# The output gate's projection between TensorE's products of the recurrence, half an item per block of tokens

## The chip, the cores and the metric

One core of a Trainium2 chip runs the kernel. The core has five engines that run side by side: TensorE (PE, matrix products; PEld is its loading of weights), VectorE (DVE), ScalarE (ACT), GpSimd (POOL) and SyncE (SP, which here issues transfers). They meet only at semaphores. The metric is the device time of one execution in microseconds (us), lower is better, as the median of several executions.

## The reference

One layer of a decoder trunk on 1024 tokens of width 1024, in float32. What matters here is its first half:

```python
xn = rmsnorm(h)
proj = xn @ w_in        # [conv value | conv gate | hgrn q | forget | input | output gate g]
# HGRN2, 4 heads of 128, in chunks of 64 tokens:
f = lb + (1 - lb) * sigmoid(z);  log_f = log(f);  k = (1 - lb) * sigmoid(-z);  q = silu(q_in)
# per chunk: inter + intra products with exp(cumsum(log_f)), state carried to the next chunk
o = rmsnorm_per_head(o) * norm_g
o = o * silu(g)         # the output gate
h = h + concat(y_conv, o) @ w_out
```

The second half (product-key retrieval over 16384 experts) and the final norm are not touched.

## The kernel before

The program is a row of stages, each a block with one instruction stream for each engine; a stage starts when all engines have ended the one before. The stages are: input norm (0 to about 59 us), the projections with the convolution (`mixer`, first block, about 59 to 293 us), the recurrence (`mixer`, second block, 294 to 450 us), the norms and the gate (`mixer`, third block, 450 to about 507 us), the output projection, the queries, the selection with the first expert layer, and the combination (to 3223 us).

**Projections.** Activations stand as two float16 parts `xh` and `xl` in `region_x`, weights as `wh` and `wl`. One item is 128 columns of the weights; one half item is that item on 512 tokens: 8 slices of the contraction with three products each (L398 to L400), 24 in all, into one PSUM bank. Items come in turns of two (ring slots s = 0, 1). SP loads an item (L80), ACT makes the high part and scales the rest (L85, L86), POOL subtracts to make the low part (L91). The order of the turns is: conv gate, conv value, forget, (input projection), q, and last the output gate, `G = (8, 10)`, whose results ACT takes through Silu into `gte` (L474, L475). While PE does this, DVE does the depthwise convolution (L553 to L565) and then four scans (L572) of the log decays.

**Recurrence.** It runs over 8 blocks of 128 tokens. In each block: DVE makes the exponents of 6 levels and of `k_end` (L622, L625); ACT takes Exp of them (L690, L691, L693); POOL multiplies the key half (L723) and DVE the query half (L636, L638); PE makes a product per level and head (L746) and one of the diagonal (L749), into PSUM banks `SCORE = (0, 1, 6, 7)` in turn; DVE copies each level under its mask into `att` (L648, seven copies). PE transposes `k_end` (L755), ACT copies it (L702), PE makes the state updates of both chunks (L762), the product with `att` (L768), and the product with the old state for chunk 0 and chunk 1 (L774). Between those two DVE makes the new state (L660), for which the second waits. ACT copies the block's output to `y` (L682). DVE makes the exponents of block n+1 before the states of block n, so DVE's order in a block is: q products, copies, exponents of the next block, states. Its buffers (levels, states and so on) are carved out of `region_x` (L578), over the activations `xh` and `xl`. After the last block POOL scales `gte` by the norm's gain (L731).

**Norms and gate.** PE takes group means (L819) and then sums of squares (L824); ACT squares (L858) and converts the output weights (L840, L841); then come root, reciprocal, spreading (L833), and DVE multiplies by `gte` (L892).

Of the kernel before, what the change touches and what calls it, by code (L numbers as in the profile page):

```python
# [6 lines left out]
P = 128  # L7
# [314 lines left out]
def mixer(nc, ctx, sb, sems, psum, region_x, y, region_k, region_w, ident, group_mean, stat, const_b, const_m,  # L322
# [16 lines left out]
    tmp = [lbs[:, (2 + i) * CG:(3 + i) * CG] for i in range(6)]  # L339

# [14 lines left out]
    BEFORE_V, TURNS, V_ITEMS = A[1], G[1], KC // 2  # L355
# [7 lines left out]
    with nc.Block() as blk:  # L363
        @blk.sync
        def _(sp):
            def load(turn, s):
                ring.load(sp, s, w_stream[ds(turn * 2 + s, 1), :, :])

            sp.dma_start(cm[:, :], const_m).then_inc(masks_in, 16)
            with sp.Fori(1, BEFORE_V) as turn:  # L370
                for s in range(2):

                    sp.wait_ge(w_lo, BASE + item(turn, s, True) - 1)
                    load(turn, s)
# [3 lines left out]
            with sp.Fori(BEFORE_V, TURNS) as turn:  # L378
                for s in range(2):
                    sp.wait_ge(w_lo, BASE + item(turn, s, False) - 1)  # L380
                    load(turn, s)
            sp.wait_ge(masks_in, 16)

        @blk.tensor
        def _(pe):
# [30 lines left out]
            turns(F[1], TURNS, False, V_TURNS)  # L416

        @blk.scalar
        def _(act):
# [54 lines left out]
            slices(G[0], G[0], silu_to(gte), True, False, V_TURNS)  # L474
            slices(G[0] + 1, G[0], silu_to(gte), False, False, V_TURNS)  # L475

        @blk.gpsimd
        def _(pool):
# [25 lines left out]
            with pool.Fori(F[1] + 1, TURNS) as turn:  # L504
                for s in range(2):
                    low(turn, s, False)
# [69 lines left out]
    used = [0]  # L576

    def carve(n):  # L578
        flat = region_x[:, :, :].rearrange("p a n -> p (a n)")
        used[0] += n  # L580
        return flat[:, used[0] - n:used[0]]

    lev = [carve(CG * P).rearrange("p (h t) -> p h t", h=CG) for _ in range(LEVELS)]
    k_end = carve(CG * P).rearrange("p (h t) -> p h t", h=CG)
    q_beg = carve(CG * P).rearrange("p (h t) -> p h t", h=CG)
    k_blk = carve(CG * P).rearrange("p (h t) -> p h t", h=CG)
    v_blk = carve(CG * P).rearrange("p (h t) -> p h t", h=CG)
    att = carve(CG * P).rearrange("p (h t) -> p h t", h=CG)
    k_end_t = carve(CG * P).rearrange("p (h t) -> p h t", h=CG)
    state = [carve(CG * P).rearrange("p (h t) -> p h t", h=CG) for _ in range(2)]  # L590
    decay = carve(3 * CG).rearrange("p (h c) -> p h c", h=CG)

    LV = LEVELS
    SCORE = (0, 1, 6, 7)
# [13 lines left out]
    with nc.Block() as blk:  # L608
        @blk.vector
        def _(dve):  # L610
# [18 lines left out]
            def intra(n):  # L629
# [11 lines left out]
                for l in range(LV + 1):  # L641
                    dve.wait_ge(sc_mm, BASE + n * (LV + 1) + (l + 1))

                    dve.wait_ge(sc_ok, BASE + n * (LV + 1) + l)

                    dve.memset(decay[:, 0:1, 2:3], 0.0)
                    mask = cm[:, l * P:(l + 1) * P].rearrange("p (a t) -> p a t", a=1).to_broadcast([P, CG, P])
                    dve.copy_predicated(att, mask, bank(SCORE[l % 4])).then_inc(sc_ok, 1)  # L648

# [27 lines left out]
        def _(act):  # L677
# [5 lines left out]

            def decays(n, first):
# [9 lines left out]
                if not first:  # L694
                    outputs(n - 1)
# [8 lines left out]
            decays(0, True)  # L704
            with act.Fori(1, TB) as n:
                decays(n, False)
# [3 lines left out]
        def _(pool):  # L710
            begin(pool, [k_mul])
            with pool.Fori(0, TB) as n:
# [15 lines left out]
                pool.tensor_tensor(k_end, k_end, k_blk, ALU.mult).then_inc(k_mul, 1)  # L728

            for c in range(CG):  # L730
                pool.tensor_scalar(gte[:, c, :], gte[:, c, :], param("hgrn_g")[:, c:c + 1], XS, ALU.mult, ALU.mult)  # L731

        @blk.tensor
        def _(pe):
            begin(pe, [sc_mm, kt_mm, u_mm, o_mm])
            pe.wait_ge(init, BASE + 1)
            with pe.Fori(0, TB) as n:
                q_blk = qry[:, :, ds(n * P, P)]
                for l in range(LV + 1):
# [3 lines left out]
                    pe.wait_ge(sc_ok, BASE + n * (LV + 1) + max(l - 3, 0))  # L743
                    for hh in range(CG):
                        if l < LV:
                            last = pe.matmul(bank(SCORE[l % 4])[:, hh, :], lev[l][:, hh, :], lev[l][:, hh, :],  # L746
                                             start=True, stop=True)
                        else:
                            last = pe.matmul(bank(SCORE[l % 4])[:, hh, :], k_blk[:, hh, :], q_blk[:, hh, :],  # L749
                                             start=True, stop=True)  # L750
                    last.then_inc(sc_mm, 1)
                pe.wait_ge(k_mul, BASE + n * (LV + 2) + (LV + 2))
# [18 lines left out]
                for c in range(2):  # L771
                    pe.wait_ge(s_ok, BASE + 2 * n + c)
# [31 lines left out]
    with nc.Block() as blk:  # L804
# [73 lines left out]
        def _(dve):  # L878
# [1017 lines left out]
```

## Time and profile before

| | us |
|---|---|
| median of 3 runs | 3220.35 (3216.92 to 3223.66) |
| the profiled execution | 3224.61 |
| its span | 3222.8 |
| PE busy | 2946.5 (91%) |
| DVE busy | 2117.0 (66%) |
| POOL busy | 1718.9 (53%) |
| ACT busy | 1109.0 (34%) |

The profiled execution is one of its own: 1.8 us of it lie outside the span, and it is 4.3 us above the median of the runs. The shares are averages over stages with different limits, so each stage is to be read by itself. "PEclk" is the clock that TensorE was granted as a share of full speed (2.4 GHz); it takes two levels, 1.00 and 0.50 (1.2 GHz), and a value between them is a mean over a stretch. A float32 product leaves two matmul records, so the four heads of one level are eight records.

### The profile page before, as it was taken

How to read it: one execution, taken by the hardware profiler on the slowest of the kernel's cores; microseconds unless marked ns; L12 is line 12 of the kernel's file. 1: busy time of each engine (PE TensorE's matmuls, PEld its weight loads, DVE VectorE, ACT ScalarE, POOL GpSimd, SP SyncE). 2: the span in 40 equal slices, each digit the busy share in tenths (PEclk: the TensorE clock that was granted, in tenths of full speed). 3: DMA queues.
4: the chain of work that ended last, by engine and by line, in shares of the span. 5: the costliest groups of instructions: out<-in, count | busy, mean ns of one | idle time of the engine just before them, and what ended most of it. 6: DMA issues, size and time to landing. Idle time of an engine off the chain costs nothing. (4 is left out here: it accounts for less than half of the span.)

```text
span 3222.8 us, 47024 instructions
## 1 busy us (share of the span) xinstructions
PE 2946.5 (91%) x15880; PEld 1644.7 (51%) x15880; DVE 2117.0 (66%) x3995; ACT 1109.0 (34%) x1480; POOL 1718.9 (53%) x1490
## 2 busy tenths in 40 slices
PE   6998779899999999899999999599989979999987
PEld 3444754455555555577777766244434424444333
DVE  2598964211777778677777753477777757777767
ACT  4333353222444444355555553221212211121212
POOL 1213442011444443455555557677887876777884
PEclk9999788999999999999999999799999989999999
DMA  3200012111333333377777777899999996999996
GB/s 114 74 26 14 0 53 85 40 39 39 105 109 114 114 114 109 126 278 249 273 249 271 249 276 248 274 321 328 334 337 340 331 327 244 322 319 326 320 323 236
DMA packets 260395, 648.59 MB, mean 201 GB/s; under 512 B 16992, under 2 KB 115552, under 8 KB 257136
## 3 DMA queue, kind: packets, MB, share of 16 engines
q1 hardware_dynamic: 186176, 378.33, 33.4%
q0 software_dynamic: 74160, 269.52, 23.6%
q8 instruction: 32, 0.52, 0.1%
q14 instruction: 27, 0.22, 0.0%
HBM read 542.39 MB, written 105.91 MB: 201 GB/s over the span
## 5 line engine op out<-in xcount | busy, mean ns | idle before, releaser
L91 POOL TENSOR_TENSOR w_low<-w_ring,w_high 128x1024 f16<-128x1024 f32 x164 | 367.4, 2241 | 1040.6 <-ACT w_ring L86 1040.5
L1664 PE MATMUL psum<-vh,wh 128*128 128x512 bf16 x1536 | 598.5, 390 | 142.5 <-POOL wl L1713 108.9
L1245 PE MATMUL psum<-region_y,w_high 128*128 128x384 f16 x2048 | 672.6, 328 | 18.1 <-POOL w_low L91 16.4
L1246 PE MATMUL psum<-region_y,w_high 128*128 128x384 f16 x2048 | 670.3, 327 | 0.0
L1247 PE MATMUL psum<-region_y,w_low 128*128 128x384 f16 x2048 | 670.3, 327 | 0.0
L1665 PE MATMUL psum<-vl,wh 128*128 128x512 bf16 x1536 | 597.3, 389 | 0.0
L1666 PE MATMUL psum<-vh,wl 128*128 128x512 bf16 x1536 | 596.4, 388 | 0.0
L1680 ACT ACTIVATE vh<-w_ring 128x1024 bf16<-128x1024 f32 x128 | 134.9, 1054 | 896.6 <-DMA w_ring<-in_v_t_dram 836.4
L1775 DVE TENSOR_TENSOR region_x<-region_x,psum 128x1024 f32<-128x1024 f32 x192 | 234.0, 1219 | 153.7 <-PE psum L1666 122.1
L1664 PEld LDWEIGHTS psum<-vh,wh 128*128 128x128 bf16 x1536 | 153.3, 100 | 344.4 <-issue 147.3
L1709 POOL TENSOR_TENSOR vl<-w_ring,vh 128x1024 bf16<-128x1024 f32 x128 | 272.8, 2132 | 40.9 <-ACT vh L1680 40.4
L1297 ACT ACTIVATE ge<-psum 128x384 f32<-128x384 f32 x256 | 125.8, 491 | 476.9 <-PE psum L1247 472.0
L1522 DVE SCALAR_TENSOR_TENSOR tk_work<-tk_work,tk_sc 128x1024 f32<-128x1024 f32 x128 | 207.4, 1623 | 118.3 <-DMA tk_work<-in_u_rows_dram,u_step_rows 117.4
L1245 PEld LDWEIGHTS psum<-region_y,w_high 128*128 128x128 f16 x2048 | 202.8, 99 | 147.9 <-issue 23.3
L1247 PEld LDWEIGHTS psum<-region_y,w_low 128*128 128x128 f16 x2048 | 201.0, 98 | 134.5 <-issue 2.9
L1246 PEld LDWEIGHTS psum<-region_y,w_high 128*128 128x128 f16 x2048 | 202.8, 99 | 126.9 <-issue 2.4
L1666 PEld LDWEIGHTS psum<-vh,wl 128*128 128x128 bf16 x1536 | 153.6, 100 | 191.6 <-issue 18.4
L1665 PEld LDWEIGHTS psum<-vl,wh 128*128 128x128 bf16 x1536 | 153.4, 100 | 186.4 <-issue 16.0
L1338 ACT ACTIVATE scores<-psum 128x512 f32<-128x512 f32 x192 | 189.8, 1095 | 138.3 <-PE psum L1277 138.3
L1713 POOL TENSOR_TENSOR wl<-at,wh 128x768 bf16<-128x768 f32 x128 | 212.3, 1659 | 1.8 <-ACT wh L1683 1.8
L1277 PE MATMUL psum<-scores 128*128 128x128 bf16 x1536 | 196.7, 296 | 4.6 <-DVE scores L1487 4.6
L1753 DVE SCALAR_TENSOR_TENSOR psum<-region_y,weight,psum 128x1024 f32<-128x1024 f32 x128 | 164.6, 1286 | 40.8 <-DMA region_y<-in_v_t_dram,step_rows 31.6
(235 smaller groups left out, 4960.3 us busy)
## 6 DMA issues: line engine op xcount, KB each, us to landing
w_ring<-in_u_t_dram SPq DMA_DIRECT2D x128, 512.0 KB
w_ring<-in_v_t_dram SPq DMA_DIRECT2D x128, 512.0 KB
acts_dram<-ge SPq DMA_DIRECT2D x128, 384.0 KB
gates_dram<-scores SPq DMA_DIRECT2D x24, 2048.0 KB
gt<-gates_dram SPq DMA_DIRECT2D x32, 1536.0 KB, 9.5
at<-acts_dram SPq DMA_DIRECT2D x32, 1536.0 KB, 13.5
w_ring<-in_w_stream_dram SPq DMA_DIRECT2D x20, 512.0 KB, 3.2
w_ring<-in_w_q_dram SPq DMA_DIRECT2D x16, 512.0 KB, 3.3
```

Source lines behind the costliest of these rows:

```text
L91: pool.tensor_tensor(self.wl[:, s, :], self.wf[:, s, :], self.wh[:, s, :], ALU.subtract).then_inc(self.w_lo, 1)
L1245: pe.matmul(a, uh[:, par, row], xh[:, n, cols], start=(n == 0), stop=False)
L1246: pe.matmul(a, uh[:, par, row], xl[:, n, cols], start=False, stop=False)
L1247: last = pe.matmul(a, ul[:, par, row], xh[:, n, cols], start=False, stop=(n == KC - 1))
L1277: last = pe.matmul(psum[:, 4 + 2 * r + b, t * P:(t + 1) * P], hot[:, r, 0, b, :, t], hot[:, r, part, b, :, t], start=(part == 2), stop=(pa ...
L1522: dve.scalar_tensor_tensor(out=row[:, r, :], in0=row[:, r, :], scalar=1.0, in1=xtok[:, :], op0=ALU.mult, op1=ALU.mult, accum_out=dots[:, j ...
L1664: pe.matmul(a, wh[:, par, c, rows], vh[:, par, c, cols], start=(c == 0), stop=False)
L1665: pe.matmul(a, wh[:, par, c, rows], vl[:, par, c, cols], start=False, stop=False)
L1666: last = pe.matmul(a, wl[:, par, c, rows], vh[:, par, c, cols], start=False, stop=(c == CPG - 1))
L1709: pool.tensor_tensor(vl[:, par, c, :], vf[:, c % 2, :], vh[:, par, c, :], ALU.subtract).then_inc(v_lo, 1)
L1713: pool.tensor_tensor(wl[:, par, c, :], at[:, par, c, :], wh[:, par, c, :], ALU.subtract).then_inc(w_lo, 1)
L1775: dve.tensor_tensor(a, a, banks, ALU.add).then_inc(y_ok, 1)
```

## The change

The output gate's two turns leave the projections. In the recurrence, PE does half an item (24 products) per block of tokens, 8 half items in 8 blocks: three products behind each of the first four levels, and twelve between the state products of chunk 0 and chunk 1. They go to PSUM bank 7, which the scores give up (`SCORE = (0, 1, 6)`). ACT copies the bank into `gte` without Silu (`gates`), one block later, before that block's output; Silu over all of `gte` comes after the last block, before the last output's copy. The items of turn 9 are loaded by SP at the start of the recurrence and converted by ACT and POOL behind blocks 2 and 4. POOL no longer scales `gte`; it scales the four columns of the gain, and DVE applies them with the gate in one instruction. Since `xh` and `xl` have to live on, the recurrence's buffers move to `glu` and to new ones. ACT's, POOL's and PE's loops over blocks are written out.

```diff
-    BEFORE_V, TURNS, V_ITEMS = A[1], G[1], KC // 2
+    BEFORE_V, V_ITEMS = A[1], KC // 2
...
-            turns(F[1], TURNS, False, V_TURNS)
+            turns(F[1], G[0], False, V_TURNS)
...
-            slices(G[0], G[0], silu_to(gte), True, False, V_TURNS)
-            slices(G[0] + 1, G[0], silu_to(gte), False, False, V_TURNS)
...
-    SCORE = (0, 1, 6, 7)
+    SCORE = (0, 1, 6)
+    NS = len(SCORE)
+    G_BANK = 7
...
+        @blk.sync
+        def _(sp):
+            for s in range(2):
+                ring.load(sp, s, w_stream[2 * (G[0] + 1) + s:2 * (G[0] + 1) + s + 1, :, :])
...
+            def gates(n):
+                _, _, c, cols = gate_half(n)
+                act.wait_ge(g_mm, n + 1)
+                act.activation(gte[:, c, cols], psum[:, G_BANK, :], ACT.Copy, scale=BACK).then_inc(g_out, 1)
...
                 if not first:
+                    gates(n - 1)
                     outputs(n - 1)
...
-            decays(0, True)
-            with act.Fori(1, TB) as n:
-                decays(n, False)
+            for n in range(TB):
+                decays(n, n == 0)
+                if n in (NH, 2 * NH):
+                    ring.high(act, n // NH - 1, G[0] + 1 + V_ITEMS // 2)
+            gates(TB - 1)
+            act.wait_ge(g_out, TB)
+            for c in range(CG):
+                act.activation(gte[:, c, :], gte[:, c, :], ACT.Silu)
             outputs(TB - 1)
...
-            for c in range(CG):
-                pool.tensor_scalar(gte[:, c, :], gte[:, c, :], param("hgrn_g")[:, c:c + 1], XS, ALU.mult, ALU.mult)
+                if n in (NH, 2 * NH):
+                    s = n // NH - 1
+                    ring.low(pool, s, item(G[0] + 1, s, False))
+            pool.tensor_scalar(hgrn_gain, param("hgrn_g"), XS, None, ALU.mult)
...
+            def gate_part(n, first, end):
+                turn, s, _, cols = gate_half(n)
+                if first == 0:
+                    pe.wait_ge(w_lo, BASE + item(turn, s, False) + 1)
+                    if n:
+                        pe.wait_ge(g_out, n)
+                for k in range(first, end):
+                    row = slice(k * P, (k + 1) * P)
+                    pe.matmul(psum[:, G_BANK, :], wh[:, s, row], xh[:, k, cols], start=(k == 0), stop=False)
+                    pe.matmul(psum[:, G_BANK, :], wh[:, s, row], xl[:, k, cols], start=False, stop=False)
+                    last = pe.matmul(psum[:, G_BANK, :], wl[:, s, row], xh[:, k, cols], start=False,
+                                     stop=(k == KC - 1))
+                if end == KC:
+                    last.then_inc(g_mm, 1)
...
-                    pe.wait_ge(sc_ok, BASE + n * (LV + 1) + max(l - 3, 0))
+                    pe.wait_ge(sc_ok, BASE + n * (LV + 1) + max(l + 1 - NS, 0))
...
                     last.then_inc(sc_mm, 1)
+                    if l < KC // 2:
+                        gate_part(n, l, l + 1)
...
                 for c in range(2):
+                    if c == 1:
+                        gate_part(n, KC // 2, KC)
                     pe.wait_ge(s_ok, BASE + 2 * n + c)
...
-                    dve.tensor_tensor(at(y, (c, h)), at(y, (c, h)), at(gte, (c - CG, h)),
-                                      ALU.mult).then_inc(gated_ok, 1)
+                    dve.scalar_tensor_tensor(out=at(y, (c, h)), in0=at(y, (c, h)),
+                                             scalar=hgrn_gain[:, c - CG:c - CG + 1], in1=at(gte, (c - CG, h)),
+                                             op0=ALU.mult, op1=ALU.mult).then_inc(gated_ok, 1)
```

How the change orders the work on PE. First the levels of a block in the kernel before (L746 is a level's four heads, L749 the diagonal, L755 the transposes; `REGISTER_ALU` and `ISA` compute the loop's addresses):

```order
508 L746 MATMUL psum<-region_x 128x128 x4
509 L741 REGISTER_ALU
510 L742 REGISTER_ALU
511 L746 MATMUL psum<-region_x 128x128 x4
512 L741 REGISTER_ALU
513 L742 REGISTER_ALU
514 L746 MATMUL psum<-region_x 128x128 x4
```

Then the same place in the changed kernel (its L781 is the level, L765 to L767 the gate's products):

```order
504 L781 MATMUL psum<-glu 128x128 x4
505 L765 MATMUL psum<-region_x,w_high 128x512
506 L766 MATMUL psum<-region_x,w_high 128x512
507 L767 MATMUL psum<-region_x,w_low 128x512
508 L781 MATMUL psum<-glu 128x128 x4
509 L765 MATMUL psum<-region_x,w_high 128x512
```

Three products of 512 columns now stand between a level and the next, four times in a block. Second, ACT behind the last block, in the kernel before (L702 is the copy of the transposed `k_end`, L682 the output's copy, L858 the first squares of the next stage):

```order
171 L702 ACTIVATE region_x<-psum 128x512
172 L705 REGISTER_ALU
173 L705 COMPARE_AND_BRANCH
174 L682 ACTIVATE region_y<-psum 128x4x128
175 L608 UNCONDITIONAL_BRANCH
176 L836 UNCONDITIONAL_BRANCH
177 L858 ACTIVATE region_x<-region_y 128x1024 x4
```

and in the changed kernel (L712, L686 and L897 are those three; L691 is `gates`, L722 the Silu):

```order
263 L712 ACTIVATE hg_rest<-psum 128x512
264 L691 ACTIVATE gte<-psum 128x512
265 L722 ACT_TABLE_LOAD
266 L722 ACTIVATE gte<-gte 128x1024 x4
267 L686 ACTIVATE region_y<-psum 128x4x128
268 L607 UNCONDITIONAL_BRANCH
269 L875 UNCONDITIONAL_BRANCH
270 L897 ACTIVATE region_x<-region_y 128x1024 x4
```

Six instructions come to stand ahead of the last output's copy. Third, POOL behind block 2, in the changed kernel (L744 ends block 2's work, L91 is the ring's low part, L733 starts block 3):

```order
64 L744 TENSOR_TENSOR glu<-glu,hg_rest 128x512
65 L91 TENSOR_TENSOR w_low<-w_ring,w_high 128x1024
66 L733 COPY hg_rest<-region_k 128x512
67 L739 TENSOR_TENSOR glu<-glu,hg_rest 128x8x32
68 L739 TENSOR_TENSOR glu<-glu,hg_rest 128x16x16
```

In the kernel before, nothing stands between the first and the third of these; L91 of the output gate's items ran in the projections.

## Rows read from the trace of the kernel before

**Rows 1.** Windows: stretch, length, busy of PE, PEld, DVE, ACT, POOL; PEclk, DMA, GB/s

```profile
251.40:292.30 40.90, 40.88 (x190) 18.34 (x188) 33.50 (x24) 10.02 (x14) 8.49 (x3) 1.00 0.04 13
312.30:424.80 112.50, 86.13 (x600) 82.70 (x600) 101.73 (x218) 39.39 (x102) 57.94 (x54) 0.82 0.00 0
450.10:471.10 21.00, 20.94 (x48) 5.95 (x48) 5.49 (x8) 17.21 (x18) 8.52 (x4) 1.00 0.42 145
476.60:504.50 27.90, 27.64 (x32) 10.46 (x32) 22.61 (x30) 17.81 (x26) 15.93 (x11) 0.50 0.06 19
```

**Rows 2.** Timeline, DVE and ACT: start, us, instruction, count [idle before <-releaser]

```profile
274.19 10.71 DVE L572 TENSOR_TENSOR_SCAN region_k<-restart,region_k 128x1024 f32<-128x1024 bf16 x4
293.82 0.48 DVE L665 MEMSET region_x<- 128x512 f32 x1 [8.92 <-PEq L363]
292.32 0.60 ACT L445 ACTIVATE gte<-psum 128x512 f32<-128x512 f32 x1 [4.58 <-PE psum L400]
```

**Rows 3.** Timeline of DVE over two blocks, and the stage's last two copies

```profile
377.59 2.10 DVE L636 TENSOR_TENSOR region_x<-region_x,region_w 128x256 f32<-128x256 f32 x6
387.24 5.28 DVE L622 TENSOR_TENSOR region_x<-region_k 128x512 f32 x6
393.59 2.32 DVE L660 SCALAR_TENSOR_TENSOR region_x<-region_x,psum 128x128 f32<-128x128 f32 x8
395.83 3.59 DVE L636 TENSOR_TENSOR region_x<-region_x,region_w 128x256 f32<-128x256 f32 x6
399.94 0.72 DVE L648 COPY_PREDICATED region_x<-cm,psum 128x512 f32<-128x512 int32 x1
406.55 4.15 DVE L622 TENSOR_TENSOR region_x<-region_k 128x512 f32 x5
443.51 0.73 DVE L648 COPY_PREDICATED region_x<-cm,psum 128x512 f32<-128x512 int32 x1
444.37 0.72 DVE L648 COPY_PREDICATED region_x<-cm,psum 128x512 f32<-128x512 int32 x1
```

**Rows 4.** Timeline of PE: state updates, last product with the state, levels

```profile
387.78 1.71 PE L762 MATMUL psum<-region_x 64*128 64x128 f32 x16 [0.77 <-ACT region_x L702]
394.75 1.10 PE L774 MATMUL psum<-region_x 128*128 128x64 f32 x8 [3.34 <-DVE region_x L660]
396.48 8.51 PE L746 MATMUL psum<-region_x 128*128 128x128 f32 x48 [0.62 <-DVE region_x L636]
```

**Rows 5.** Windows of granted clock: levels at half and at full, and two gaps

```profile
396.50:402.20 5.70, 5.70 (x27) 5.70 (x28) 5.08 (x12) 0.72 (x3) 1.62 (x2) 0.50 0.00 0
402.60:406.30 3.70, 3.70 (x34) 3.48 (x32) 2.70 (x9) 0.00 (x0) 0.24 (x1) 1.00 0.00 0
1070.40:1078.00 7.60, 5.28 (x33) 3.22 (x34) 7.11 (x17) 4.64 (x5) 4.17 (x2) 1.00 0.34 121
1266.00:1272.80 6.80, 4.46 (x18) 2.22 (x18) 6.17 (x12) 4.18 (x4) 4.33 (x3) 0.76 0.39 135
```

**Rows 6.** Timeline of POOL and DVE in the first block

```profile
296.23 6.57 POOL L723 TENSOR_TENSOR region_x<-region_x 128x256 f32<-128x256 f32 x6 [1.99 <-ACT region_x L691]
301.05 4.86 DVE L636 TENSOR_TENSOR region_x<-region_x,region_w 128x256 f32<-128x256 f32 x6
```

**Rows 7.** Timeline of ACT and POOL: the ring's conversions and a table load

```profile
273.04 1.05 ACT L86 ACTIVATE w_ring<-w_ring 128x1024 f32<-128x1024 f32 x1
274.16 4.23 POOL L91 TENSOR_TENSOR w_low<-w_ring,w_high 128x1024 f16<-128x1024 f32 x1 [8.23 <-ACT w_ring L86]
210.05 1.28 ACT L470 ACT_TABLE_LOAD   x1
```

**Rows 8.** Timeline of PE and ACT: end of the recurrence, start of the norm stage

```profile
447.26 1.90 PE L774 MATMUL psum<-region_x 128*128 128x64 f32 x16
449.19 0.60 ACT L682 ACTIVATE region_y<-psum 128x512 f32<-128x512 f32 x1 [4.70 <-PE psum L774]
450.08 3.90 ACT L858 ACTIVATE region_x<-region_y 128x1024 f32<-128x1024 f32 x4 [0.29 <-PEq L608]
```

More of the change, by code:

```diff
@@ L339, in mixer @@
     tmp = [lbs[:, (2 + i) * CG:(3 + i) * CG] for i in range(6)]
+    hgrn_gain = tmp[0]
     masks_in = sems("masks_in")
@@ L377, in _ @@
                 sp.dma_start(wf[:, j % 2, :], w_v[j, :, :]).then_inc(w_in[j % 2], 16)
-            with sp.Fori(BEFORE_V, TURNS) as turn:
+            with sp.Fori(BEFORE_V, G[0] + 1) as turn:
                 for s in range(2):
@@ L503, in _ @@
                                    ALU.mult, ALU.mult).then_inc(key_ok, 1)
-            with pool.Fori(F[1] + 1, TURNS) as turn:
+            with pool.Fori(F[1] + 1, G[0] + 1) as turn:
                 for s in range(2):
@@ L572, in _, with gate_half @@
                 dve.tensor_tensor_scan(logf[:, c, :], restart[:, :], logf[:, c, :], 0.0, ALU.mult, ALU.add)
[L576 to L591, printed above, removed]
-    LV = LEVELS
-    SCORE = (0, 1, 6, 7)
+    in_glu = glu[:, :, :].rearrange("p c n -> p (c n)")[:, 0:8 * CG * P].rearrange(
+        "p (i h t) -> p i h t", i=8, h=CG)
+    hg_rest = sb(ctx, "hg_rest", [P, 6, CG, P], F32)
+    lev = [in_glu[:, i] for i in range(LEVELS)]
+    k_end, q_beg = in_glu[:, LEVELS], in_glu[:, LEVELS + 1]
+    k_blk, v_blk, att, k_end_t = (hg_rest[:, i] for i in range(4))
+    state = [hg_rest[:, 4 + i] for i in range(2)]
+    decay = sb(ctx, "hg_decay", [P, CG, 3], F32)
+    LV = LEVELS
+    SCORE = (0, 1, 6)
+    NS = len(SCORE)
+    G_BANK = 7
+    g_mm, g_out = sems("gate_mm"), sems("gate_out")
+    def gate_half(n):
+        c, h = divmod(n, NH)
+        return G[0] + c // 2, c % 2, c, slice(h * HALF, (h + 1) * HALF)
     init = sems("hg_init")
@@ L647, in intra @@
                     mask = cm[:, l * P:(l + 1) * P].rearrange("p (a t) -> p a t", a=1).to_broadcast([P, CG, P])
[L648 removed]
+                    dve.copy_predicated(att, mask, bank(SCORE[l % NS])).then_inc(sc_ok, 1)
             def states(n):
@@ L711, in _ @@
             begin(pool, [k_mul])
-            with pool.Fori(0, TB) as n:
+            for n in range(TB):
                 kb = key[:, :, ds(n * P, P)]
@@ L736, in _ @@
             pe.wait_ge(init, BASE + 1)
-            with pe.Fori(0, TB) as n:
+            def gate_part(n, first, end):
[12 more added lines that the diff above has]
+                    last.then_inc(g_mm, 1)
+            for n in range(TB):
                 q_blk = qry[:, :, ds(n * P, P)]
@@ L742, in _ @@
                         pe.wait_ge(k_mul, BASE + n * (LV + 2) + (l + 2))
-                    pe.wait_ge(sc_ok, BASE + n * (LV + 1) + max(l - 3, 0))
+                    pe.wait_ge(sc_ok, BASE + n * (LV + 1) + max(l + 1 - NS, 0))
                     for hh in range(CG):
                         if l < LV:
-                            last = pe.matmul(bank(SCORE[l % 4])[:, hh, :], lev[l][:, hh, :], lev[l][:, hh, :],
+                            last = pe.matmul(bank(SCORE[l % NS])[:, hh, :], lev[l][:, hh, :], lev[l][:, hh, :],
                                              start=True, stop=True)
                         else:
-                            last = pe.matmul(bank(SCORE[l % 4])[:, hh, :], k_blk[:, hh, :], q_blk[:, hh, :],
+                            last = pe.matmul(bank(SCORE[l % NS])[:, hh, :], k_blk[:, hh, :], q_blk[:, hh, :],
                                              start=True, stop=True)
                     last.then_inc(sc_mm, 1)
+                    if l < KC // 2:
+                        gate_part(n, l, l + 1)
                 pe.wait_ge(k_mul, BASE + n * (LV + 2) + (LV + 2))
```

## The prediction

> **What bounds the kernel now.** I read the time stage by stage, since the change touches the projections, the recurrence and the start of the norm stage. First the windows [rows 1]: in 251.4 to 292.3 us PE does nothing but the output gate's turns, 190 of its 192 products recorded in 40.9 us, 0.215 us each, at clock 1.00. Then the timeline at the hand-over [rows 2]: DVE's scans end at 274.19 + 10.71 = 284.90, ACT's last Silu at 292.32 + 0.60 = 292.92, and the recurrence starts at 293.82. So PE bounds the end of this stage, but DVE (convolution and scans) is only 8.0 us behind it. Of 41 us taken off PE the stage can give back 8.0.
>
> Then the recurrence. The six blocks from 312.3 to 424.8 take 112.5 us, 18.75 each; DVE is busy 101.7 of it, PE 86.1 with 100 records a block, at a mean clock of 0.82 [rows 1]. I call T the moment at which the states of a block are done and its q products start, and E the start of the next block's exponents. On DVE [rows 3], E to T is 387.24 to 395.83 = 8.6 us; T to E is 377.59 to 387.24 = 9.65 us in one block and 395.83 to 406.55 = 10.72 in the next, so periods of 18.2 and 19.3 alternate. In the longer one the q products take 3.59 us against 2.10.
>
> On PE [rows 4], the product with the new state waits 3.34 us for DVE: there the twelve gate products fit. The levels start 0.65 us after T (396.48). Their pace depends on the clock [rows 5]: at 0.50, 27 records in 5.70 us, 0.211 each; at 1.00, 34 in 3.70, 0.109 each. A level is eight records: 1.7 us or 0.9. After the 3.34 us gap the levels ran at half clock for 5.7 us; after the 0.77 us wait for ACT the state updates (L762, 16 records in 1.71, 0.107 each) went on at full [rows 4].
>
> **The change part by part**, as differences to the profiled execution.
>
> *Projections, -8.0.* The gate's turns go; late next is DVE's last scan. With the same 0.9 us from the last instruction to the next stage, the recurrence starts at 285.8 instead of 293.82 [rows 2]. This is nearly certain: -7.5 to -8.5.
>
> *Does the clock hold?* In each block PE gets 12 products x 0.215 = 2.6 us into the 3.34 us gap, and 4 x 3 x 0.215 = 2.6 us among the levels. Its work per block at full clock is 100 x 0.109 + 5.2 = 16.1 of about 19 us, and the waits left are 0.77 (ACT), 0.7 before the state product and 0.62 before the levels [rows 4]. The 0.7: PE ended chunk 0's product at 394.75 - 3.34 = 391.4, E + 4.2; with 2.6 more it is E + 6.8, and the state, which DVE starts at 393.59 [rows 3], is there at 394.75, E + 7.5. Two gaps of about 2 us in another stage bracket this: around 1070.4 to 1078 the mean clock stayed 1.00, in 1266 to 1272.8 it fell to a mean of 0.76 [rows 5]. Mine are shorter than both, so I take the clock as held from block 1 on.
>
> *Score phase, blocks 1 to 6: +1.5.* At full clock: first level at T + 0.65; seven products (six levels and diagonal) x 0.9 = 6.3; four gate groups x 0.65 = 2.6; so PE ends at T + 9.55, the last copy (0.72, [rows 3]) starts about 0.15 later, and E = T + 10.4. DVE by itself would take, with the slower q products, 395.83 to 399.94 = 4.1 and seven copies at the pitch of 444.37 - 443.51 = 0.86: 10.1. PE is late by a little. The period is 8.6 + 10.4 = 19.0 against 18.75: +0.25 x 6 = +1.5. What full clock gives is spent on the gate groups. With three score banks instead of four, level 3 waits for copy 0, done at T + 4.1 + 0.7 = 4.8; PE reaches level 3 at T + 0.65 + 2.7 + 1.95 = 5.3, so this costs nothing; if PE were 0.5 us quicker it would bind. Bounds: -0.75 per block (all like the 9.65 block, [rows 3]), that is -6 over eight blocks, and for the other end rival B.
>
> *Block 0: +2.4.* PE has stood idle since the projections, so it starts at half clock, as before (0.50 over levels, [rows 5]). A stretch of 5.7 us at half costs half of it, 2.85; with 0.4 for the first q product beside POOL [rows 6], T to E is 10.4 + 2.85 + 0.4 = 13.65; before it was 301.05 [rows 6] to 312.3, 11.25. Bounds 0 and +3.5.
>
> *ACT and POOL at blocks 2 and 4: +2.0.* The ring's two ACT passes are 1.05 each, and POOL's subtraction 4.23 / 2 = 2.1 [rows 7]. POOL waits for ACT's, and block n+1's key products (6.57 us, [rows 6]) queue behind POOL's: they start some 4 us later and run on past T. PE doesn't wait for them, since level l needs only product l. But DVE's q products then run beside them: 4.86 us as in block 0 [rows 6] instead of 3.59, +1.27, of which the 0.3 that DVE is ahead of PE absorbs some: +1.0, twice. Bounds 0 (hidden) and +2 x 2.1 (POOL's whole subtraction shows). ACT's 2.1 us lie in its waiting (ACT is busy 39 of 112.5 us, [rows 1]); `gates`, 0.6 a block, runs while ACT waits for the output (4.70 us idle behind block 7, [rows 8]). The two loads fall where DMA moves nothing [rows 1]: nothing.
>
> *Behind block 7: +7.2.* Nothing hides anything here. Before: PE's two state products back to back from 447.26, 1.90 for both; ACT's copy 449.19 + 0.60 = 449.79 ends the stage [rows 8]. After: first product to 448.2; twelve gate products, +2.6 = 450.8; `gates` 0.6 = 451.5 with a tenth for the semaphore; table load 1.28 [rows 7] = 452.8; four Silu of 128x1024, as the four squares 3.90 [rows 8] = 456.7; the output's copy 0.6 = 457.3. That is +7.5, less 0.3 because PE's last levels end earlier at full clock. Bounds +6 and +8.5.
>
> What the Trainium skill says of the table load speaks for more: its page "ScalarE: Activation LUTs", section "What ACT_TABLE_LOAD costs", puts a drain beside the load, about 2.7 us for a switch. The row shows 1.28 for the load alone, and by the page this term would be +8.6 instead of +7.2.
>
> *Norm stage: +2.4.* PE does 48 records in 21.0 us without a pause and the root waits for the last [rows 1]; at the start, before, the clock was full. Now PE idles from its last product (about 451.7 on the old scale) to 457.6, more than any gap above that held, so it starts at half: half of 5.7 us = 2.85, less about 0.4 in which ACT was the later one. Bounds +1.3 and +3.4. The gating on DVE takes one more scalar per instruction, cost nothing: PE is busy 27.6 of 27.9 us there at clock 0.50, DVE 22.6 [rows 1]; without that cover 8 x 0.1 us. POOL's L731 goes from a stretch where PE, at half clock, was the later one: nothing.
>
> Sum: -8.0 + 1.5 + 2.4 + 2.0 + 7.2 + 2.4 = **+7.5**. Against the profiled 3224.6 us that is 3232.1; that execution is 4.3 above the median of 3220.35, so the median forecast is 3227.9. A difference under 0.2% (6.4 us) can't be told from none.
>
> **Rivals.**
>
> *B, the clock still falls in the recurrence.* Place: PE between chunk 0's state product and the next levels. If the waits left add up so that the clock drops as before, the levels and the gate groups run at half for 5.7 us of each such block, +2.85: in every second block +10, in all seven +20, so 3238 to 3248. For it: the 1266 window, where a gap of about 2 us was enough [rows 5]. Against it: my gaps are about 0.7 each. The Trainium skill ("TensorE: Matmul & The Clock Gate", section "A second HAM failure mode: psum-queue depth-cycling") tells of a kernel whose frequent short PE pauses made the clock swing, without one long one; the held 1070 window speaks against it here. Chance 0.17.
>
> *C, not slower: DVE carries the score phase.* Place: L746 to the last copy. In the full-clock levels PEld is busy 3.48 of 3.70 us [rows 5], so a gate product's 0.215 us may cover the next float32 weight load and a group cost 0.4 instead of 0.65. It decides once the last level ends before T + 9.2; then E is DVE's 10.1 (-0.3 x 8 = -2.4), and if the q products also take the short form, 9.65: -0.75 x 8 = -6.0, and the ring's 2.0 gone. 3220 to 3225.5, at best 3219.9. Against it: full clock lets POOL start its copies right at T, as in the longer blocks. Chance 0.23.
>
> *A, the sum above,* 0.60; its own range is 3222 to 3234 by its terms, 0.38 of it beyond +6.4 and 0.22 within.
>
> **Numbers.** Slower: 0.38 + 0.17 = 0.55. Same: 0.22 + 0.15 of C = 0.37. Faster: 0.08, the low end of C with a cheaper tail. The range 3217 to 3240 holds A, nearly all of C and the near half of B.
>
> **What would show it.** Right: the recurrence begins at about 286; block periods near 19.0 without alternation; mean clock near 1.00 over blocks 1 to 6; blocks 3 and 5 about 1 us longer; PE's wait before the state product about 0.7; table load and four Silus, some 7 us, between PE's last product and the next stage; PE at 0.50 as that starts. Wrong: a clock of 0.8 or less in the blocks and periods over 21 (B); periods of 18.5 or less with no copy waiting for PE (C); the term for the tail under 5, or a first norm stretch at clock 1.00.

## The result, and the profile after

| kernel | median (us) | runs | profiled execution | its span |
|---|---|---|---|---|
| before | 3221.0 | 8 (3216.9 to 3223.7) | 3224.61 | 3222.8 |
| after | 3229.2 | 8 (3226.4 to 3234.4) | 3234.42 | 3232.6 |

The ratio is 1.0027, with a 95% interval of 1.0016 to 1.0038: 8.2 us slower, where 7.5 was forecast. The profiled executions' spans differ by 9.8 us, and that is the sum taken apart here; the profiled one of after is the slowest of its eight, 5.2 us above their median. Medians were taken on four occasions, and the kernel before measured 3221.0, 3222.9, 3227.7 and 3223.8 us on them. So runs of different occasions are compared by their ratios to it, and not by their medians.

The windows of the changed kernel (columns as in [rows 1]) show one block with a fall of the clock (block 1), one without (block 6), six blocks together, the tail, and the norm stage's start; the last two are the stretch at half clock in block 1, and the levels behind it:

```profile
305.20:325.70 20.50, 18.53 (x124) 14.66 (x124) 17.62 (x38) 7.17 (x19) 9.16 (x10) 0.92 0.00 1
408.60:427.40 18.80, 16.87 (x124) 13.60 (x124) 17.60 (x37) 7.13 (x19) 9.13 (x10) 1.00 0.00 1
305.20:427.40 122.20, 109.41 (x744) 87.35 (x744) 109.35 (x217) 45.97 (x113) 58.45 (x57) 0.93 0.00 1
427.40:459.30 31.90, 23.93 (x176) 19.09 (x176) 19.99 (x45) 13.82 (x26) 8.93 (x10) 0.99 0.00 1
459.50:482.00 22.50, 22.44 (x46) 6.93 (x47) 5.50 (x8) 18.39 (x19) 9.38 (x5) 0.87 0.41 143
...
315.40:318.70 3.30, 3.30 (x14) 2.33 (x13) 3.22 (x7) 0.00 (x0) 0.67 (x1) 0.51 0.00 0
319.00:323.90 4.90, 4.90 (x40) 4.33 (x39) 2.57 (x7) 0.00 (x0) 0.00 (x0) 1.00 0.01 3
```

The six blocks took 122.2 us where they took 112.5 [rows 1], and DVE's busy time grew with them (101.7 to 109.4). Nearly all of that is in the q products: 17.1 us in the six blocks before, where three blocks had the short ones of 2.10, and 24.8 us now, where none has. The mean clock rose from 0.82 to 0.93, but not to the 1.00 on which the forecast counted: it fell once in each of blocks 1 to 5, to 0.51 (the 1.2 GHz level) for about 3.3 us, and the period (from the start of a block's exponents to the next block's) was 20.5 us, with the ring's work 21.0; block 6, without a fall, took 18.8.

On DVE, the scans, the recurrence's first instruction, the q products of three blocks, and the starts of blocks 2 and 7:

```profile
274.86 8.83 DVE L571 TENSOR_TENSOR_SCAN region_k<-restart,region_k 128x1024 f32<-128x1024 bf16 x4
284.60 0.48 DVE L669 MEMSET hg_rest<- 128x512 f32 x1 [0.91 <-PEq L364]
...
313.78 3.58 DVE L640 TENSOR_TENSOR glu<-glu,region_w 128x256 f32<-128x256 f32 x6
321.73 0.73 DVE L652 COPY_PREDICATED hg_rest<-cm,psum 128x512 f32<-128x512 int32 x1 [0.81 <-DVE hg_rest L652]
325.69 5.28 DVE L626 TENSOR_TENSOR glu<-region_k 128x512 f32 x6
...
354.96 5.21 DVE L640 TENSOR_TENSOR glu<-glu,region_w 128x256 f32<-128x256 f32 x6
...
427.43 5.28 DVE L626 TENSOR_TENSOR glu<-region_k 128x512 f32 x6
```

The recurrence begins at 284.60 instead of 293.82 [rows 2]: 9.2 us earlier. The 0.81 us idle before the copy at 321.73, though put down to DVE's own buffer, is time in which no levels were there to copy: PE was at half clock until 318.7, and a level with its gate group takes it 1.54 us even after that (the copies at 320.19, 321.73 and 323.27 are that far apart). The q products of block 3 take 5.21 us.

PE around the gap of block 2, whose clock fell at 335.75:

```profile
333.19 1.10 PE L813 MATMUL psum<-glu,hg_rest 128*128 128x64 f32 x8 [0.83 <-DVE hg_rest L664]
334.74 1.23 PE L781 MATMUL psum<-glu 128*128 128x128 f32 x8 [0.45 <-DVE glu L640]
```

Of the 3.34 us before the product with the state [rows 4], 0.83 is left (0.7 was forecast); 0.45 before the levels. Blocks 1, 4, 6 and 7 have the same two waits within 0.01 us, and in blocks 6 and 7 the clock held; blocks 3 and 5, with the ring's work, have 1.04 and 0.78.

The tail and the start of the norm stage, on ACT:

```profile
452.97 0.60 ACT L691 ACTIVATE gte<-psum 128x512 f32<-128x512 f32 x1 [6.32 <-PE psum L767]
453.58 1.28 ACT L722 ACT_TABLE_LOAD   x1
454.88 3.89 ACT L722 ACTIVATE gte<-gte 128x1024 f32<-128x1024 f32 x4
458.68 0.57 ACT L686 ACTIVATE region_y<-psum 128x512 f32<-128x512 f32 x1
459.53 3.89 ACT L897 ACTIVATE region_x<-region_y 128x1024 f32<-128x1024 f32 x4 [0.28 <-PEq L607]
...
479.07 1.06 ACT L879 ACTIVATE region_w<-w_ring 128x1024 f16<-128x1024 f32 x1 [1.90 <-DMA w_ring<-in_w_out_dram]
482.58 0.59 ACT L902 ACTIVATE glu<-psum 16x512 f32<-16x512 f32 x1 [0.21 <-PE psum L863]
```

Block 7 starts at 427.43 and the norm stage 32.1 us later; before it was 424.78 and 25.3. Nothing covers the load, the four Silu and the copy. The root comes 23.05 us into the stage, before 22.6.

### The profile page after: what moved, and what is told of

Read it like the earlier page. It is cut to its first block and busy times, and to the rows that moved or that the text cites. A ratio compares the mean times of both kernels' runs of the same rounds, so it can differ in the third digit from the quotient of the medians.

```text
span 3232.6 us, 46622 instructions
## 1 busy us (share of the span) xinstructions
PE 2941.5 (91%) x15880; PEld 1633.5 (51%) x15880; DVE 2123.6 (66%) x3995; ACT 1112.7 (34%) x1485; POOL 1712.0 (53%) x1487
## 5 line engine op out<-in xcount | busy, mean ns | idle before, releaser
L91 POOL TENSOR_TENSOR w_low<-w_ring,w_high 128x1024 f16<-128x1024 f32 x164 | 364.0, 2220 | 1049.0 <-ACT w_ring L86 1049.0
```

Of the source, the lines that this page charges most:

```text
L91: pool.tensor_tensor(self.wl[:, s, :], self.wf[:, s, :], self.wh[:, s, :], ALU.subtract).then_inc(self.w_lo, 1)
```

## The experiments

The diffs are shortened to the lines that matter. The main theory, H: PE's clock falls at the waits that are left and costs 1.65 us a time; with the waits filled it holds. Its rival: the new order itself makes the blocks 20.5 us long. "Behind E7" is the time from block 7's start to the norm stage, E and T are the prediction's.

**e1: three more products in each gap.** They are repeats and compute nothing that is used.

```diff
  gate_part(n, KC // 2, KC)
+ for _ in range(3):
+     pe.matmul(psum[:, 2, :], wh[:, gate_half(n)[1], 0:P],
+               xh[:, 0, 0:HALF], start=True, stop=True)
```

> The changed kernel with three more products of 512 columns (0.65 us) that nobody uses, into PSUM bank 2, in PE's wait before the state product of chunk 1 (0.82 us in the profile). Theory H: in blocks 1 to 5 the clock fell for 3.3 us of each block because of the waits left around the state product (0.82 and 0.44 us), and each fall costs half of 3.3 us. Then with the wait filled the clock stays at 1.00 in all blocks, the periods of 20.5 become 18.8 as in block 6, and the time falls by 5 x 1.65 = 8 us (about 3221). Rival P: the 20.5 is the order of PE's work (levels queue behind gate products) and the clock a by-product; then periods stay 20.5 and the time the same within 2 us.

Measured: 3226.1 us, ratio 1.0014 (1.0005 to 1.0023), with more work on PE than in after. Its six blocks, and PE in blocks 2 and 3:

```profile
303.38:419.69 116.31, 105.58 (x762) 83.25 (x762) 109.32 (x217) 46.00 (x113) 58.47 (x57) 1.00 0.00 1
```

```profile
329.70 1.11 PE L815 MATMUL psum<-glu,hg_rest 128*128 128x64 f32 x8 [0.17 <-DVE hg_rest L664]
331.25 0.94 PE L781 MATMUL psum<-glu 128*128 128x128 f32 x6 [0.44 <-DVE glu L640]
...
356.42 1.13 PE L781 MATMUL psum<-glu 128*128 128x128 f32 x8 [0.91 <-DVE hg_rest L652]
```

With 0.17 us left of the wait (0.39 in the ring's blocks) the clock is 1.00 in all six blocks, and four of the six periods are 18.8. H stands, and the order of work alone (P) is out. The other two, with the ring's work, are 20.5: there PE waits 0.91 us for DVE to copy a score bank. So the ring costs 1.7 us a time where the clock is held; in after it showed as 0.5, beside a fall. That is why the six blocks are only 5.9 us shorter than in after's profile (116.31 for 122.2) and not 8. In the median, expected about 3221, it is less still: from a ratio of 1.0027 to 1.0014, about 4 us, and the two intervals overlap.

**e2: seven eighths of the Silu before the end**, in ACT's wait of block 7.

```diff
+ if last:        # behind block 7's decay
+     act.wait_ge(g_out, TB - 1)
+     # Silu of gte[:, 0:CG-1, :] and gte[:, CG-1, 0:HALF]
...
- # gates(TB - 1), four Silu of 128x1024
+ act.activation(gte[:, CG - 1, HALF:T], psum[:, G_BANK, :], ACT.Silu, scale=BACK)
```

> The changed kernel with seven of the eight halves of Silu (and the table load) taken while ACT waits for the transposes in the last block (8.8 us idle), and the last half directly from PSUM. Theory T: behind the last block nothing hides ACT, so table load 1.28 and Silu 3.9 are paid in full: the stage end comes 5.2 us earlier, time -5.2; PE's pause before the norm stage shrinks from 6 to about 1.5 us, so that stage may start at full clock and give back up to 1.7 more. Rival: what comes earlier is lost in the norm stage's waits for the output weights, time the same within 2 us.

Measured: 3227.8 us, ratio 1.0020 (1.0011 to 1.0029). ACT in the tail:

```profile
436.73 1.28 ACT L713 ACT_TABLE_LOAD   x1
438.02 2.95 ACT L713 ACTIVATE gte<-gte 128x1024 f32<-128x1024 f32 x3
440.88 0.61 ACT L714 ACTIVATE gte<-gte 128x512 f32<-128x512 f32 x1
...
452.38 0.60 ACT L725 ACTIVATE gte<-psum 128x512 f32<-128x512 f32 x1 [6.32 <-PE psum L770]
453.22 0.60 ACT L686 ACTIVATE region_y<-psum 128x512 f32<-128x512 f32 x1 [0.24 <-PE psum L816]
```

Behind E7 it is 27.25 us instead of 32.1: 4.85 saved (5.2 expected). The ratio is 0.0007 below after's, some 2 us, and the intervals overlap. The tail's size is shown, its whole worth in the total is not.

The second half of the expectation can be read too. Here PE's pause was short and the norm stage ran at full clock from its start to its root:

```profile
454.10:476.97 22.87, 20.94 (x48) 5.99 (x48) 5.51 (x8) 18.76 (x19) 9.76 (x5) 1.00 0.43 141
```

It took 22.87 us, where after's took 23.05 with its first 6 us at half clock. So the fall at this place cost next to nothing, and not the 1.7 that were expected back.

**e3: a smaller share among the levels**, three slices instead of four; five in the gap.

```diff
- if l < KC // 2:      gate_part(n, l, l + 1)
+ if l < IN_LEVELS:    gate_part(n, l, l + 1)      # IN_LEVELS = 3
- gate_part(n, KC // 2, KC)
+ gate_part(n, IN_LEVELS, KC)
```

> The changed kernel with five slices of the gate (15 products, 3.2 us) between the two state products and three among the levels, instead of four and four. Theory H: the wait before the state product shrinks from 0.82 to 0.17 us, the clock holds, and the level phase is 0.65 us shorter, so that DVE bounds it (10.1 us from states to exponents): periods of 18.6, time -8 to -10. Rival P (the order of work alone): -0.65 x 7 = -4.5, periods 19.8, clock still falling.

Measured: 3226.6 us, ratio 1.0007 (0.9998 to 1.0016), not told from before; against after it is some 6 us (the two intervals only touch), where 8 to 10 were expected. The clock is 0.99 over six blocks: it fell once, in block 3, where the ring's work had lengthened the two waits to 1.29 and 0.89 us (block 5 has the same waits, and no fall). Four periods are 18.5, and the two with the ring 21.0 (block 3) and 20.4. T to E is 9.95 us: with one group fewer PE is no longer the late one, and DVE sets the pace (rival C's place).

```profile
304.41:419.96 115.55, 103.12 (x744) 82.25 (x744) 109.48 (x217) 46.83 (x113) 58.61 (x57) 0.99 0.00 1
```

**e4: the kernel before with its gap filled**, by 14 products that compute nothing.

```diff
  for c in range(2):
+     if c == 1:
+         for _ in range(14):
+             pe.matmul(psum[:, 2, :], wh[:, 0, 0:P], wl[:, 0, 0:HALF], start=True, stop=True)
```

> The kernel before with 14 products of 512 columns (3.0 us) that nobody uses, into PSUM bank 2, in PE's 3.34 us wait before the state product; everything else as before. It prices the clock's fall in the kernel before. If levels at half clock hold up DVE's copies there, the periods fall from 18.75 to DVE's own 8.6 + 10.0 = 18.6 or less, clock 1.00: time -1 to -3 us. If the shorter q products of every second block were due to the half clock (POOL starting its copies later), they go as well and the periods become 18.6 all alike. If products in the wait delay the state product, the time rises by 0.3 per block, +2.

Measured: 3224.6 us, ratio 1.0005 (0.9996 to 1.0014).

```profile
312.64:423.75 111.11, 94.13 (x693) 78.47 (x695) 105.71 (x218) 39.92 (x102) 54.64 (x54) 0.97 0.00 0
```

The alternation of 18.2 and 19.3 is gone: every period is 18.5. The clock still fell in blocks 3, 5 and 7, but for 3.4 us instead of 6.8, and these blocks are no longer than the others. How the alternation came about can be read in the trace of the kernel before, at T of block 4 (the state product on PE, and POOL's copy behind it) and of block 5 (POOL's copy):

```profile
376.51 1.97 PE L774 MATMUL psum<-region_x 128*128 128x64 f32 x8 [3.33 <-DVE region_x L660]
```

```profile
378.66 1.49 POOL L726 COPY region_x<-region_w 128x512 f32 x1 [1.74 <-PE psum L774]
396.04 0.67 POOL L726 COPY region_x<-region_w 128x512 f32 x1 [0.88 <-PE psum L774]
```

Where the clock had fallen before the state product, that took 1.97 us instead of 1.10 [rows 4], POOL's copy waited for it and started 1.07 us behind the q products' start (378.66 for 377.59, [rows 3]) instead of 0.21, and the q products, mostly without POOL beside them, took 2.10 us instead of 3.59. Such a block took 18.2 us, less than the 18.5 of e4 without a fall; where the clock fell behind the state product, the levels took 8.5 us [rows 4], and the block 19.3. The clock's fall so helped by holding POOL back, or cost by slowing the levels, depending on where it began. (In e7 the short q products come once more, and that block is not shorter, so this holds for the kernel before only.) The gain of the filled wait over six blocks is only 1.4 us (111.11 for 112.5), and behind E7 the same products show as +2.5 (27.8 for 25.3). Half clock cost the old kernel little, since DVE carried its blocks.

**e6: no ring work in the recurrence.** It leaves out the loads and conversions of turn 9 and uses another turn's weights in its place. One execution only.

```diff
- item(turn, s, False)
+ item(G[0], s, False)     # and ring.high, ring.low, two loads removed
```

> The changed kernel without the loads and conversions of turn 9 in the recurrence; PE uses turn 8's items twice, so half of the gate's values are left out. The two blocks behind the conversions had q products of 5.2 us instead of 3.6 and periods of 21.0 against 20.5 here, and 20.53 against 18.81 where the wait was filled. Theory R: POOL, pushed back by ACT's two passes and its own subtraction, works beside DVE's q products; then all q products are 3.6 and blocks 3 and 5 have the period of their neighbours (20.5 at a falling clock, 18.8 at a held one). Rival: the longer periods come with the position in the clock's rhythm, and stay.

Measured: 3242.5 us, span 3240.7. DVE and POOL in block 3, and the six blocks:

```profile
354.14 3.58 DVE L639 TENSOR_TENSOR glu<-glu,region_w 128x256 f32<-128x256 f32 x6
```

```profile
347.13 6.34 POOL L735 TENSOR_TENSOR glu<-glu,hg_rest 128x256 f32<-128x256 f32 x6 [1.50 <-ACT glu L699]
```

```profile
304.61:427.45 122.84, 111.14 (x744) 88.71 (x744) 105.56 (x217) 42.89 (x109) 54.91 (x55) 0.92 0.00 1
```

Here the clock fell in all seven blocks and every period was 20.5, blocks 3 and 5 too. The q products took 3.58 us instead of 5.21, so it is the ring's work that pushes POOL's key products beside them. Of the 1.6 us that DVE saves, 0.5 shows in the period (20.5 for 21.0), since PE, at half clock, is late anyway, and a sixth fall among the six blocks took more than both gave. The total says nothing about the ring: 2779.5 us of the span lie behind the start of the norm stage, 6.4 more than in after's profile, in code that is the same.

**e5_again: after once more**, no edit.

> The changed kernel itself, once more. In its first profile the clock fell in blocks 1 to 5 and not in 6; in the run with one more subtraction beside the scans, whose blocks have the same code, it held in blocks 1, 2, 3 and 5. If where it falls is chance of the single execution (gaps of 0.82 and 0.44 us lie at the edge), the set of blocks differs here again, with 1.7 us for each: between no fall (a recurrence 8 us shorter than in the first profile) and a fall in all seven. If it is fixed by the code, blocks 1 to 5 fall again.

Measured: 3233.3 us (3225.6 to 3235.0), ratio 1.0031 (1.0021 to 1.0042). Its profile has falls in blocks 1, 2 and 3 only and a span of 3227.4:

```profile
303.96:424.04 120.08, 106.35 (x744) 85.16 (x744) 109.33 (x217) 45.98 (x113) 58.46 (x57) 0.96 0.00 1
```

The same instructions give three falls in one execution and five in another, with the same waits. So the number of falls is a matter of the execution; the waits make a fall possible and do not fix it. The width of its times (8.0 and 9.5 us) can't be put down to the falls: e1, whose profile has none in its blocks, spreads over 12.3 us, and the kernel before over 6.7 to 12 us. (The expectation has the blocks of e8 wrong: there the clock held in blocks 1 to 4.)

**e7: the change by halves.** Turn 9 and half of turn 10's gate work go back to the projections; blocks 0 to 3 alone carry four slices each, in the gap only. No ring work in the recurrence, no tail.

```diff
- gate_part(n, l, l + 1)                 # among the levels
- gate_part(n, KC // 2, KC)              # in the gap
+ if n < 4: gate_part(n, 4 * (n % 2), 4 * (n % 2) + 4)
```

> The changed kernel with six of the eight half items back in the projections (PE is idle there from 252 to 284 us, six halves take 31), through Silu as before, and two left for the recurrence, as 12 products in the wait before the state product of blocks 0 to 3, none among the levels; no conversions in the recurrence; the last item's Silu while ACT waits in block 7. From the terms measured so far: start -8 (scans beside POOL again, 10.7 instead of 8.8, so not -9.2), blocks as in the kernel before or, where the wait is filled, 18.5 instead of 18.75 (-1), no tail, no ring. Time against the kernel before: -9, about 3213. If the gain at the start is given back later, it is 0.

Measured: 3220.7 us (3213.5 to 3221.9), ratio 0.9974 (0.9965 to 0.9984), with 3227.7 for the kernel before on the same occasion. Windows, then ACT at the end:

```profile
304.35:415.74 111.39, 89.74 (x649) 78.82 (x649) 104.67 (x218) 41.29 (x105) 56.09 (x55) 0.92 0.00 1
```

```profile
426.49 1.28 ACT L724 ACT_TABLE_LOAD   x1
427.79 1.06 ACT L724 ACTIVATE gte<-gte 128x1024 f32<-128x1024 f32 x1
...
439.59 0.60 ACT L696 ACTIVATE region_y<-psum 128x512 f32<-128x512 f32 x1 [4.62 <-PE psum L818]
```

Periods are 18.53 to 18.56, once 18.68, though the clock is 0.92 as in e6 (it fell in blocks 1, 4, 5, 6 and 7): with nothing among the levels, a fall costs next to nothing. Behind E7 it is 24.7 us. The start keeps 7.9 of its 9.2 us. This beats both kernels, by 0.26% or about 8 us against before, where 9 were expected.

**e9: e7 with the gaps of all seven blocks filled** by 2 or 14 empty products.

```diff
+ for _ in range(14 if n in (4, 5, 6) else 2 if n < 4 else 0):
+     pe.matmul(psum[:, 2, :], wh[:, 1, 0:P], xh[:, 0, 0:HALF], start=True, stop=True)
```

> The split kernel with products that nobody uses (14 in blocks 4 to 6, two more in blocks 0 to 3) in PE's wait before the state product, so that it is filled in every block but the last. Theory H: clock 1.00 and periods 18.5 in all blocks: 0.25 less in each of three to seven blocks, -1 to -2 against the split kernel, -10 against the kernel before. Rival: no more than the split kernel, since periods with a fallen clock alternate between 18.2 and 19.3 anyway.

Measured: 3217.9 us, ratio 0.9972 (0.9963 to 0.9981).

```profile
304.53:415.78 111.25, 92.67 (x685) 76.37 (x685) 105.86 (x217) 41.32 (x105) 54.99 (x55) 0.98 0.00 1
```

The clock is 0.98 instead of 0.92 (one fall, in block 6), and the six blocks take 111.25 us instead of 111.39: the same. The 1 to 2 us of theory H did not come. The clock mattered only where PE was late.

**e8: a POOL subtraction put back beside the scans** (one execution, on after; its output is not used).

```diff
+ pool.wait_ge(conv, BASE + CG * TAPS)
+ pool.tensor_tensor(gte[:, 0, :], key[:, 0, :], key[:, 1, :], ALU.subtract)
```

> The changed kernel with one more subtraction of 128x1024 on POOL, of values that nobody uses, started when DVE starts its four scans. The scans took 10.71 us before, when POOL made the last low parts beside them (one instruction, 4.23 us instead of 2.1), and 8.83 in the changed kernel, when POOL was idle. Theory S: they slow one another, so the scans take 10 to 11 us here and POOL's subtraction 3 to 4. Rival: the 1.9 us are not POOL's doing (the convolution's end moved, ACT and PE were busy too), and the scans stay at 8.8.

Measured: 3236.8 us, span 3235.0. DVE, then POOL, then a subtraction of the same size 10 us ahead of the scans, in the kernel before:

```profile
274.96 10.93 DVE L573 TENSOR_TENSOR_SCAN region_k<-restart,region_k 128x1024 f32<-128x1024 bf16 x4
```

```profile
275.12 4.26 POOL L507 TENSOR_TENSOR gte<-region_k 128x1024 f32<-128x1024 f32 x1 [17.94 <-DVE region_y L566]
```

```profile
263.80 2.13 POOL L91 TENSOR_TENSOR w_low<-w_ring,w_high 128x1024 f16<-128x1024 f32 x1 [8.14 <-ACT w_ring L86]
```

One POOL instruction makes the scans 2.1 us longer (8.83 to 10.93), as much as such a subtraction takes away from them, and is twice as long beside them (4.26 for 2.13). In this execution the clock fell in blocks 5, 6 and 7 only.

**e10: e7 with its last POOL subtraction moved** from beside the scans into block 0.

```diff
- ring.low(pool, 1, item(G[0] + 1, 1, False))      # end of the projections
+ if n == 0: ring.low(pool, 1, item(G[0] + 1, 1, False))   # behind the first k_blk copy
```

> The split kernel with POOL's last low part moved from beside DVE's scans (3.99 us there, scans 10.7) into the recurrence, behind POOL's first copy, where POOL waits 2.2 us for ACT's first exponentials. Theory S: the scans take 8.8, the recurrence starts 1.9 us earlier, POOL's subtraction 2.1 us, hidden; time -1.9 against the split kernel, about -10.5 against the kernel before. If POOL's key products of block 0 are pushed on and DVE's q products slowed beside them, up to 1 us of it is lost.

Measured: 3213.3 us, ratio 0.9973 (0.9964 to 0.9982), not told from e7.

```profile
273.63 8.83 DVE L587 TENSOR_TENSOR_SCAN region_k<-restart,region_k 128x1024 f32<-128x1024 bf16 x4
...
284.31 6.54 DVE L637 TENSOR_TENSOR glu<-region_k 128x512 f32<-128x512 f32 x6
```

```profile
283.60 2.11 POOL L91 TENSOR_TENSOR w_low<-w_ring,w_high 128x1024 f16<-128x1024 f32 x1
```

The scans give back 1.9 us, and the first exponents, now beside the subtraction, take 6.54 us where they take 5.22 in block 0 elsewhere; the subtraction itself, which started first, keeps its 2.11. Block 0 is 1.3 us longer (18.85 for 17.52). It was expected to be hidden, and is not: most of the cost moves with the instruction.

## Why the prediction was right, and where its steps were not

| term | forecast | measured in the profile |
|---|---|---|
| projections | -8.0 | -9.2 |
| block 0 | +2.4 | +2.2 |
| score phase, six blocks | +1.5 | +0.4 |
| clock | 0 (held) | +8.3 |
| ring, twice | +2.0 | +1.0 |
| behind block 7 | +7.2 | +6.8 |
| norm stage | +2.4 | +0.4 |
| sum | +7.5 | +9.9 |

Block 0 runs from the start of its exponents to block 1's: 19.67 us (285.54 to 305.21) where it took 17.51. Blocks 1 to 6 took 122.2 us; six times the 18.82 of block 6, where nothing fell, is 112.9, against 112.5 before; five falls of 1.65 (20.47 less 18.82) are 8.3; what remains is the ring's 1.0. The terms add up to the difference of the spans within their rounding.

*Projections, right with more than forecast.* The row of 4.23 us in [rows 7] is one instruction, not two. The forecast halved it to 2.1 and missed what it said: POOL was slowed beside the scans, so the scans were slowed too. After has no POOL work there, and they take 8.83 us instead of 10.71; e8 brings both numbers back. The convolution ends 0.7 later in this profile, which leaves 1.2 of the 1.9; that is scatter, since it ended between 273.67 and 274.86 in the profiles of after, e5_again and e1, which have the same code there. The 2.1 for a subtraction away from the scans was right by luck (2.13, see e8); in the recurrence, beside DVE's exponents, it took 2.70 (348.53).

*"I take the clock as held": the step that failed.* The waits left were as forecast (0.83 and 0.45 us for 0.7 and 0.62), but the two stretches of [rows 5] bracket nothing. Their gaps, which stand here in the first product behind each, are as good as equal, and the longer one is the one that held:

```profile
1072.72 0.33 PE L1245 MATMUL psum<-region_y,w_high 128*128 128x384 f16 x1 [2.39 <-POOL w_low L91]
1268.43 0.33 PE L1245 MATMUL psum<-region_y,w_high 128*128 128x384 f16 x1 [2.34 <-POOL w_low L91]
```

So the length of a single gap did not decide there, and a shorter gap was no promise. What differs in after is two waits 1.1 us apart, in every block; e1, which shortens the first to 0.17, held the clock in all its blocks. Which feature of the pair matters was not separated, and why the clock held in blocks 6 and 7 with the same waits stays open. So rival B's mechanism happened in five blocks of seven. Its price of 2.85 was too high, since half clock lasted 3.3 us here and not 5.7; the 1266 window of [rows 5] already had it, a mean of 0.76 over 6.8 us being 3.3 us at half. Nor did the clock fall in every second block before: it fell in each, for 6.8 us (in block 5 from 395.8 to 402.7). The Trainium skill ("TensorE: Matmul & The Clock Gate", section "A second HAM failure mode: psum-queue depth-cycling") tells of a kernel in which short pauses of TensorE between groups of products, when frequent enough, made the clock swing. The trace of after agrees, with waits of 0.83 and 0.45 us.

*Score phase, right.* PE is late by a little: 18.82 for the forecast 19.0 at full clock. e3 shows the turning point: one group less and DVE is the late one, at 18.53.

*Ring, right in place.* The q products run beside POOL's key products and take 5.2 us. Its price depends on the clock: 0.5 beside a fall, 1.7 without (e1), where the copy of a score bank makes PE wait. So with the clock held, as the forecast had it, the ring is 3.4 for the forecast 2.0. The forecast had let three score banks cost nothing ("if PE were 0.5 us quicker it would bind"); in those blocks DVE was that much later instead.

*Tail, right:* 6.8 for 7.2, and e2 takes 4.85 of it away. The load took 1.28 us, started where the copy before it ended, and the first Silu started 1.30 behind its start, so no further time for a switch shows. The 2.7 us of the Trainium skill ("ScalarE: Activation LUTs", section "What ACT_TABLE_LOAD costs") would have made this term worse.

*Norm stage, too high by 2: the second step that failed.* The mean clock there was 0.87, so it did start at half, for 6 us. But ACT waits 1.90 us for w_out at 479.07 and was the later one by more than the 0.4 assumed; PE's lost time lay beside that wait. Two profiles with this stage at full clock bear it out: 22.87 us to the root (e2) and 23.55 (e7), for 23.05 (after) and 23.62 (e1) with the half clock at its start. The clock makes no difference here that stands out from the scatter.

**Luck in the total.** It was close because errors met: 8.3 us of falls that were not in the sum, against 5.9 by which the other six terms together came out lower. Had the clock held, as assumed, the sum of this profile would be 9.9 less the 5.9 of e1, which is 4.0; and e1 measured a ratio of 1.0014, about 4.5 us. That is slower clear of the noise, on the tail, block 0 and the start, which came nearly as worked out. But it is less than the 0.2% (6.4 us) below which the forecast itself saw no telling from none. So the way was right by its reasons, and the size of 7.5 by the falls.

## What to carry to other kernels

Filling one engine's waits with work is worth only what the place it came from gives up, which is bounded by the next engine there (9 us of 41 here), and what lands behind the recurrence, where nothing covers it, is paid in full. Put such work only into the wait, not into the phase in which that engine sets the pace, and leave the last pieces where they were: the half move (e7) gained 0.26% where the whole move lost 0.27%. Before work is added or left in for the sake of the clock, ask whether that engine is late at all: filling the gap in a kernel carried by DVE (e4, e9) bought nothing that could be told. And before two stretches are used as bounds, look whether they differ in the thing that is to be bounded: here two gaps of one length had opposite outcomes.

## What the runs showed of the hardware

- Two waits of 0.83 and 0.45 us, 1.1 us of work apart, let TensorE's granted clock fall to 0.51 for 3.3 us, but not each time: blocks with the same two waits held it. How often it falls differs between executions of the same program (five blocks in one, three in another). A single gap of 2.34 us was followed by a fall, one of 2.39 us was not.
- VectorE's four scans of 128x1024 take 8.83 us without GpSimd work beside them and 10.7 to 10.9 beside one GpSimd subtraction, which itself takes 3.7 to 4.3 us instead of 2.1 (before, e7, e8, e9). Six products of 128x256 took 2.10 us when GpSimd's copy started 1.07 us behind them, 3.58 when it started with them, and 5.2 beside GpSimd's key products. Six exponent instructions took 5.22 us, or 6.54 beside a subtraction that had started first and kept its 2.11.
